# Two key jobs of the next layer, moved from the router gaps into the expert quads

## The reference, cut to what matters

```
for l in range(2):
    h = h + mixer(rms_norm(h, norm_mix[l])) @ w_out[l]
    m = rms_norm(mem, norm_mem[l])
    k, v = m @ xa_wk[l], m @ xa_wv[l]          # 256x1024 by 1024x1024 each
    h = h + attention(rms_norm(h, norm_cross[l]) @ xa_wq[l], k, v) @ xa_wo[l]
    t = rms_norm(h, norm_ffn[l])
    combine = top-1 of 4 groups, then top-2 of its 8 experts, with weights
    for e in range(32):
        h = h + combine[:, e] * ((silu(t @ w_gate[e]) * (t @ w_up[e])) @ w_down[e])
out = rms_norm(h, final_norm)
```

## Time and profile before

| | us |
|---|---|
| median of 3 runs (1002.92 to 1005.67) | 1004.59 |
| the profiled execution | 1003.95 |
| its span in the profile | 1002.2 |
| PE busy in the span | 865.3 (86%) |
| DVE busy | 329.8 (33%) |
| ACT busy | 161.9 (16%) |
| HBM read 268.71 MB, written 1.05 MB over the span | 269 GB/s in the mean |

### The profile page before, as it was taken

How to read it: one execution, slowest core, us unless ns; L and a number is a source line. 1 busy time by engine, 2 the same in 40 slices (tenths; PEclk the granted TensorE clock), 3 DMA queues, 4 the chain that set the end, 5 groups by cost and what they waited for, 6 DMA issues and landing times.

```text
span 1002.2 us, 11960 instructions
## 1 busy us (share of the span) xinstructions
PE 865.3 (86%) x5080; PEld 564.8 (56%) x5080; DVE 329.8 (33%) x649; ACT 161.9 (16%) x381; POOL 15.2 (2%) x21
## 2 busy tenths in 40 slices
PE   3999998889999997878877999898999699787674
PEld 3888876559757534335525888655974554333121
DVE  3105755332224322112112575543122432222114
ACT  3200122511211100000011021342121010000002
POOL 5000000000000000000000000000000000000000
PEclk9999999999999999999998999999999699989888
DMA  9543543133449999999995344323544699999993
GB/s 357 192 168 116 175 174 149 70 121 131 169 187 346 430 427 426 428 428 426 428 422 238 132 157 170 155 86 124 213 169 188 259 428 420 428 428 428 428 427 154
DMA packets 22940, 270.63 MB, mean 270 GB/s; under 512 B 2912, under 2 KB 3296, under 8 KB 5216
## 3 DMA queue, kind: packets, MB, share of 16 engines
q1 hardware_dynamic: 21152, 267.35, 65.7%
q10 hardware_dynamic: 1728, 2.42, 0.8%
HBM read 268.71 MB, written 1.05 MB: 269 GB/s over the span
## 4 chain that ended last, share of the span: by engine, by line
PE 58%; DMA 22%; issue 6%; PEld 6%; DVE 5%; ACT 4%; DVEq 0%; SPq 0%; PEldq 0%; ACTq 0%
DMA ring<-in_expert_units 21%; PE bank L489 16%; PE bank L557 11%; PE bank L852 6%; PE bank L543 5%; PE bank L593 3%; PE bank L580 2%; PE bank L623 2%; PEld bank L580 2%; PE bank L638 2%; PE bank L884 1%; PE bank L865 1%; PE bank L680 1%; PEld bank L489 1%; PE bank L510 1%
## 5 line engine op out<-in xcount | busy, mean ns | idle before, releaser
L593 PE MATMUL bank<-ring,xT 128*32 128x512 f32 x944 | 126.3, 671 | 61.7 <-DMA ring<-in_expert_units 61.6
L489 PE MATMUL bank<-uT,ring 128*128 128x256 f32 (+1 forms) x512 | 114.3, 382 | 2.5 <-DVE uT L1325 2.5
L593 PEld LDWEIGHTS bank<-ring,xT 128*32 128x32 f32 x944 | 30.4, 117 | 149.9 <-issue 95.1
L489 PEld LDWEIGHTS bank<-uT,ring 128*128 128x128 f32 (+1 forms) x512 | 94.4, 187 | 18.9 <-DVE uT L1325 3.0
L1755 DVE TENSOR_TENSOR hid<-hid,bank 128x256 f32<-128x256 f32 x16 | 6.7, 421 | 189.5 <-ACT hid L1226 189.5
L638 PE MATMUL bank<-yy,turned 128*128 128x512 f32 x128 | 63.6, 619 | 2.2 <-DVE h L1769 2.2
L557 PE MATMUL bank<-ring,uT 128*128 128x512 f32 x128 | 57.8, 608 | 7.2 <-DVEq L1613 7.2
L580 PE MATMUL bank<-sel,hn 128*128 128x128 f32 x512 | 62.3, 282 | 2.0 <-DVE sel L1731 1.7
L580 PEld LDWEIGHTS bank<-sel,hn 128*128 128x128 f32 x512 | 60.8, 198 | 2.5 <-DVE place L1722 1.9
L852 PEld LDWEIGHTS bank<-uT,ring 128*128 128x128 f32 x512 | 57.8, 192 | 1.1 <-DVE uT L1325 0.5
L852 PE MATMUL bank<-uT,ring 128*128 128x128 f32 x512 | 57.8, 275 | 0.0
(11 more groups left out here) (280 smaller groups left out, 955.1 us busy)
## 6 DMA issues: line engine op xcount, KB each, us to landing
ring<-in_expert_units SPq DMA_DIRECT2D x87, 2048.0 KB, 21.0
ring<-in_fixed_units SPq DMA_DIRECT2D x16, 2048.0 KB, 7.9
ring<-in_fixed_units SPq DMA_DIRECT2D x26, 1024.0 KB, 13.8
early<-in_expert_units SPq DMA_DIRECT2D x9, 2048.0 KB, 7.8
ring<-in_fixed_units SPq DMA_DIRECT2D x2, 768.0 KB, 4.3
kT<-in_mem SPq DMA_DIRECT2D x2, 512.0 KB, 5.5
h<-in_x SPq DMA_DIRECT2D x1, 1024.0 KB, 10.2
ring<-in_fixed_units SPq DMA_DIRECT2D x2, 512.0 KB, 3.3
```

Source lines behind the costliest of these rows:

```text
L489: mm = pe.matmul(o[row0:row0 + m], w[:, c, c0:c0 + m], rhs[:, c], start=(c == 0), stop=(c == chunks - 1))
L593: mm = pe.matmul(bank[2][32 * e:32 * e + 32, :], xT[:, 2 * n + c, 32 * e:32 * e + 32], w[:, e, :, c], start=(n == 0 and c == 0), stop=(n = ...
```

## The change

Layer 1's router gap loses the four key tiles, and the jobs xk0 and xk1 move into quads 2 and 3; the jobs that were in quads 3 to 6 move by one or two places, so that quads 2 to 7 have one each. The ring order changes with it: expert unit 0 now follows out0, unit 1 follows out1, 2 and 3 follow xq0 and xq1, 4 and 5 follow xout0 and xout1; the first unit of quad 1 still follows expert unit 0, and early 3 is still issued after router1.

```
-NEXT_BEFORE_STEP, NEXT_IN_QUAD, NEXT_BEHIND_LAYER = ["xk0", "xk1"], {3: "xk2", 4: "xk3", 5: "xv0", 6: "xv1"}, ["xv2", "xv3"]
+NEXT_IN_QUAD, NEXT_BEHIND_LAYER = {2: "xk0", 3: "xk1", 4: "xk2", 5: "xk3", 6: "xv0", 7: "xv1"}, ["xv2", "xv3"]
...
-RING_ORDER = [(0, name) for name in KEYS_VALUES + OTHERS] + [(1, name) for name in NEXT_BEFORE_STEP] + expert_ring_units(0)
+RING_ORDER = [(0, name) for name in KEYS_VALUES + OTHERS] + expert_ring_units(0)
...
-JOBS += [(1, "xk0", "A", 4), (0, "places", "V", 7), (1, "xk1", "A", 5)]
+JOBS += [(0, "places", "V", 7)]
...
-                if before == "xk0" and (of, lay) == (1, 0) or of == 1 and before == 0:
+                if before == 0:
                     sp.wait_ge(pe_job, INDEX[lay, "router1"] + 1)
                     load_early(lay, 3)
...
                 router(0)
-                if lay == 0:
-                    pe.wait_ge(next_gained, 1)
-                    wait_unit(base, "xk0", 1)
-                    k0 = begin("xk0", 1)
-                    key_tile(1, "xk0", k0, 0, memN)
                 transposes("ffn", hn, 1)
                 router(1)
-                if lay == 0:
-                    key_tile(1, "xk0", k0, 1, memN).then_inc(pe_job, 1)
-                    wait_unit(base, "xk1", 1)
-                    k1 = begin("xk1", 1)
-                    key_tile(1, "xk1", k1, 0, memN)
-
                 pe.wait_ge(M["r_chosen"], in_layer(lay, "r_chosen", 1))
...
-                if lay == 0:
-                    free_unit("xk0", 1)
-                    key_tile(1, "xk1", k1, 1, memN).then_inc(pe_job, 1)
-                    free_unit("xk1", 1)
-
-
                 after("places")
...
                     if name is not None:
+                        pe.wait_ge(next_gained, 1)
                         fill_next(name, base)
-                    if lay == 0 and q == 0:
-                        wait_emptied(1, "xk1")
                     down(q, base, units_of(q, 4, 6), name)
...
-                if lay == 0:
-                    keep_memory(1, "xk0")
                 act.wait_ge(M["r_exp"], in_layer(lay, "r_exp", 2))
                 act.activation(rt[:, 112:114], rt[:, 112:114], ACT.Exp).then_inc(M["r_exp_e"], 1)
                 load_tables(SILU_TABLES)
-                if lay == 0:
-                    keep_memory(1, "xk1")
```

## The result

The changed kernel takes 1014.3 us (median of 4 runs, 1013.48 to 1015.89) beside 1003.75 for the kernel before in the same comparison: ratio 1.0106, 95% interval 1.0083 to 1.0129. A second comparison, later and on another occasion, gave 1013.39 beside 1005.40: 1.0078, interval 1.0060 to 1.0095. Slower by 8 to 10.5 us; the forecast was 1012.3, and the two medians are 2.0 and 1.1 us above it. The profiled execution took 1013.48 us, its span is 1011.7.

What follows compares the result with a forecast made beforehand. The prediction took the expert stages to be bound by DMA transfers, with TensorE work between them covered. It added 5.4 (stream) and 3.0 (quad 7), 8.4 us, to 1003.95 for 1012.3 us, range 1006.5 to 1015.5.

Steps and rivals of the forecast that it cites:

- step 1: Layer 1's router gap: VectorE's chain and a cold TensorE replace four key tiles (14.3 us); no earlier expert stage booked.
- The template from layer 2: Layer 2's 34.5 us from early 2's issue to the issue expert unit 0's release allows, taken over for layer 1: 322.6.
- The rival in which the clock holds by itself: Layer 1's router gap: the clock stays up without key tiles, so only quad 7 costs: 1007.1 us, chance 0.06.
- A: The experiments' theory for layer 1's gap: stream idle until up(0) frees its first buffer, a release the cold TensorE delays.
- step 2: Layer 1's expert stream: new transfer order makes the last unit ready at 528.8 instead of 523.44, +5.4 us.
- T: The last landing of a transferred unit in layer 1's expert stage, forecast at 528.8.
- step 3: Quads 2 to 6 of layer 1's expert stage: the jobs stay covered by the transfer stream, zero cost.
- step 4: Quad 7 of layer 1: xv1's job ends behind the last landing and delays down(7), +3.0 us.
- the tail: Time by which work behind T holds up the end of layer 1's stage; forecast at +3.0 us.
- a rival of chance 0.08: Quad 7: a cold TensorE runs the last gate unit and part of xv1 at half speed, +1.5 up to +2.4 us.
- step 5: The rest: xv2's unit a gate unit later, changed waits, two fewer ACT copies in the gap; zero each.
- The rivals with a time of 1007 and below: Clock holds in layer 1's gap, 1007.1, chance 0.06; holds in both gaps, 1001.9, or falls late in both, 1007.1, together 0.06.

Runs made afterwards that it cites:

- e6: The changed kernel with xv1 behind xv0 in quad 6, so quads 1 and 7 have no job: 1009.21 us, ratio 1.0037 to the kernel before.
- e7: e6 with unread matmuls (4, 9 and 3) in both layers' router gaps: 999.87 us, ratio 0.9943 to the kernel before.
- e1: The changed kernel with unread matmuls (4, 12 and 3) in layer 1's router gap: 1010.42 us, ratio 1.0050 to the kernel before.
- the second profile: The changed kernel run once more, unaltered: 1013.39 us, ratio 1.0078 to the kernel before.
- e8: The changed kernel with 5 unread matmuls behind each of the second and third gate units of layer 1's quad 7: 1016.63 us, ratio 1.0099.
- e9: e8 once more, unaltered: 1016.15 us in its one run.
- The square: Layer 1 stage ends, tail excluded. Old order: 237.2 clock up (before), 238.2 clock falling (e2). New order: 237.5 up (e7), 242.9 falling (e6).
- e4: The changed kernel with its six jobs one quad earlier, in quads 1 to 6: 1011.35 us, ratio 1.0069 to the kernel before.
- e2: The kernel before, with each of the gap's four key tiles computing one of its eight chunks: 1004.65 us, ratio 0.9993.
- e3: The kernel before, with job xv1 and its unit moved from quad 6 to quad 7: 1009.62 us beside 1005.54, ratio 1.0049.

## Why the prediction was right, and where it was off

1. *The gap (step 1).* Right in kind: up(0) starts where it did, behind VectorE's chain and a cold TensorE. The template from layer 2 gave a release at 34.5; the first profile has 33.3 (gather 5.20 us, as the clock was back at 1.00 in 318 to 320), the second 34.5 and e6 34.8. The page "TensorE: Matmul & The Clock Gate" of the Trainium skill (Part 1) says that activity is what releases the throttle. e6 and e7 agree: same order of units, none or 16 matmuls that nobody reads, gather 6.44 or 3.81 us. e1 shows that activity did not always suffice: the clock was 0.50 in 306 to 308 with TensorE at work. The rival in which the clock holds by itself did not occur; where it was made to hold (e7), A was gone, 0.3 us left.

2. *The stream (step 2).* +5.4 was forecast for T; e6 has +5.7, the second profile +5.6, the first +4.2. The step's second half, 186.6 + 19.6 = 206.2 us from the release to T, held almost exactly: 206.1 to 206.4 in all seven profiles that have the new order and no job in quad 1 (both of the changed kernel, e1, e6, e7, e8, e9), while their releases lie between 29.3 and 35.0. So a us at the release is a us at T. I treated the step as one sum. The square shows the two things in it: the new order leaves the stream nothing to do until the release, and the cold clock puts the release 5 us later. Each alone costs 1 us or less.

3. *Quads 2 to 6 (step 3).* Zero, and right: e6 has two jobs in quad 6 and takes the same 206.3 us from the release to T. What the cover is worth shows in e4, where quad 1 has no such cover: 209.2 us, 3 us more for a job of 7.

4. *Quad 7 (step 4).* The mechanism was right, the size off: the term "+3.0 us" of the tail measured 4.5 and 4.6. The sum used the last gate unit at 1.92 us; it ran 3.5 us, since the clock had fallen while TensorE waited between gate units that come 4.9 us apart. Where it ran at 1.92 us (e8, e9), the tail was 3.0. I had this as a rival of chance 0.08, priced rightly at +1.5 and up; it should have been part of the forecast, as in the kernel before the gate unit just ahead of the last one already took 3.42 us:

```profile
508.85 3.42 PE L593 MATMUL bank<-ring,xT 128*32 128x512 f32 x16 [2.88 <-DMA ring<-in_expert_units]
513.65 1.92 PE L593 MATMUL bank<-ring,xT 128*32 128x512 f32 x16 [1.38 <-DMA ring<-in_expert_units]
```

   There, TensorE still waited 1.33 us for T, so a slow gate unit is mostly covered: in e2, whose quad 7 has no job, the last gate unit took 3.58 us and the stage ended 0.1 us over T + 1.85. With xv1 behind it, it is not covered. The profiled execution is 9.5 us over the one before, and 8.4 was forecast: the tail adds 1.5, the stream's 4.2 instead of 5.4 takes 1.2 back, and 0.8 come from outside the stage. That the total is so near is partly luck.

5. *The rest (step 5).* Zero held for the order of xv2's unit and for ACT. In the first profile xv2 starts 0.2 us later relative to the scatter and takes 0.6 us longer, both within what the profiles differ by.

The rivals with a time of 1007 and below asked for a clock that holds in a 5.4 us wait. In all six profiles with an empty gap in layer 1 it fell, and in layer 2 in every profile without filler.

## What to carry to other kernels

In a stage that is bound by transfers, look at when its first buffer is released: here what stood in front of that release, a cold TensorE too, was paid in full, unless other transfers could go meanwhile. Work moved into such a stage was free only in the quads where TensorE waited for transfers; 3 us of 7 were paid in a quad where it didn't, and 3.0 to 5.1 behind the last transfer. A wait of 5 us that no useful work fills can be worth filling with matmuls nobody reads, sized just below the wait (here 5.2 us of the stage for 16 of them).

## What the hardware showed that was not expected

- A filled gap doesn't always hold the clock. In e1 it fell to 0.50 in 306 to 308 with TensorE busy all through, behind router1's narrow matmuls; in e3 32 key matmuls took 8.84 us where 7.15 is usual (0.57 in 304 to 308), and in e7's layer 2 the 9 matmuls took 5.80 us instead of 4.13 (0.50 in 782 to 784).
- The first 128 recorded key matmuls of the program take 27.9 us in some executions and 29.4 to 30.9 in others, all of kernels that are alike there. That is part of the 3.6 us by which the profiles differ at early 2's issue.
- Ten more matmuls in quad 7 went with 8.2 and 8.5 us of stand at the end of the stage instead of 4.3 to 4.8, in both runs of that kernel, and with a second block of instructions brought in meanwhile. No run tests whether the one causes the other.
